# The loads of the down weights of the list of expert units go out from ACT's queue instead of SyncE's

## The reference

```python
def swiglu(h, w_gate, w_up, w_down):
    return (jax.nn.silu(h @ w_gate) * (h @ w_up)) @ w_down
...
    _, eidx = lax.top_k(masked, TOP_K)            # 8 of 64 experts for each token
    ...
    routed = routed_experts(xf, eidx, wts, w_e_gate, w_e_up, w_e_down)
    return routed + swiglu(xf, w_s_gate, w_s_up, w_s_down)
```

## Time and profile before

| | |
|---|---|
| median of 3 runs | 3423.13 us (3420.48 to 3427.93) |
| the profiled execution's own time | 3420.63 us |
| span of its records | 3418.5 us |
| mean granted TensorE clock | 0.869 of full speed |
| PE busy | 2907.1 us (85%) |
| DVE, ACT, POOL busy | 926.5, 652.5, 170.2 us |
| read from HBM, written | 604.84 MB, 47.71 MB |

### The profile page before, as it was taken

The page is one execution under the profiler, slowest core; times in us unless marked ns, Lnnn a source line. Parts: engine busy times, 40 slices in busy tenths (PEclk is TensorE's granted clock), DMA queues, the critical chain, the costliest instruction groups (busy, mean ns, idle before and its releaser), DMA issues.

```text
span 3418.5 us, 39374 instructions
## 1 busy us (share of the span) xinstructions
PE 2907.1 (85%) x16028; PEld 1537.9 (45%) x16028; DVE 926.5 (27%) x2134; ACT 652.5 (19%) x1282; POOL 170.2 (5%) x178
## 2 busy tenths in 40 slices
PE   6867997888999899989897688897888989887885
PEld 3333344666444544434343334344657874332333
DVE  0232443333111432111112421343343142111113
ACT  2232222221100201111110232222222011111111
POOL 0000000000000011111110000000000001111100
PEclk8998578767999889999999799578778989999997
DMA  5100003212120249999996510002110338999994
GB/s 248 67 1 31 0 25 124 75 75 75 49 77 22 82 191 377 422 395 413 372 409 257 205 55 7 25 25 100 51 75 29 145 141 325 419 422 419 413 410 167
DMA packets 74563, 617.38 MB, mean 181 GB/s; under 512 B 17678, under 2 KB 17678, under 8 KB 32016
## 3 DMA queue, kind: packets, MB, share of 16 engines
q1 hardware_dynamic: 50192, 564.49, 40.6%
q0 software_dynamic: 24192, 50.39, 3.9%
HBM read 604.84 MB, written 47.71 MB: 191 GB/s over the span
## 4 chain that ended last, share of the span: by engine, by line
PE 77%; DVE 12%; issue 4%; DMA 3%; ACT 3%; SPq 0%; DVEq 0%; POOLq 0%; ACTq 0%; POOL 0%
PE bank L1595 18%; PE bank L1610 8%; PE bank L1081 7%; PE bank L271 7%; PE bank L342 3%; PE bank L1096 2%; PE bank L1086 2%; PE bank L1585 2%; PE bank L562 2%; PE bank L570 2%; DMA arena<-expert_rows 2%; PE bank L363 1%; PE bank L383 1%; PE bank L401 1%; PE bank L792 1%
## 5 line engine op out<-in xcount | busy, mean ns | idle before, releaser
L1595 PE MATMUL bank<-ring,arena 128*64 128x512 f32 (+1 forms) x1648 | 587.1, 631 | 101.4 <-issue 96.7
L1595 PEld LDWEIGHTS bank<-ring,arena 128*64 128x64 f32 (+1 forms) x1648 | 203.6, 158 | 423.6 <-issue 422.5
L1081 PE MATMUL bank<-normed,ring 128*128 128x512 f32 (+1 forms) x768 | 255.5, 486 | 0.0
L1595 PE MATMUL bank<-branches,arena 128*64 128x512 f32 (+1 forms) x528 | 249.8, 629 | 0.0
L1773 DVE TENSOR_TENSOR arena<-bank,arena 128x256 f32<-128x256 f32 x83 | 35.2, 425 | 705.0 <-ACT arena L1697 705.0
L271 PE MATMUL bank<-normed,ring 128*128 128x512 f32 x512 | 223.4, 598 | 1.3 <-DVE branches L477 1.3
L1519 POOL DMA_INDIRECT arena<-hidden_rows,block_slots x81 | 82.2, 1015 | 2800.4 <-DVE block_slots L1348 2194.4
L1081 PEld LDWEIGHTS bank<-normed,ring 128*128 128x128 f32 x768 | 145.9, 190 | 102.2 <-issue 92.3
L1610 PE MATMUL bank<-ring,arena 128*64 128x512 f32 (+1 forms) x560 | 163.4, 597 | 1.3 <-DVE arena L1779 1.3
L1697 ACT ACTIVATE arena<-bank 128x256 f32<-128x256 f32 x83 | 31.9, 384 | 687.6 <-PE bank L1595 687.6
L271 PEld LDWEIGHTS bank<-normed,ring 128*128 128x128 f32 x512 | 98.1, 192 | 123.9 <-issue 122.1
(11 more groups left out here) (369 smaller groups left out, 4077.3 us busy)
## 6 DMA issues: line engine op xcount, KB each, us to landing
ring<-in_wexp SPq DMA_DIRECT2D x96, 2048.0 KB, 11.1
ring<-in_wst SPq DMA_DIRECT2D x54, 2048.0 KB, 7.7
branches<-in_wexp SPq DMA_DIRECT2D x34, 2048.0 KB, 11.5
ring<-in_wexp SPq DMA_DIRECT2D x66, 1024.0 KB, 11.1
arena<-in_wexp SPq DMA_DIRECT2D x64, 1024.0 KB, 21.5
arena<-expert_rows SPq DMA_DIRECT2D x12, 2048.0 KB, 7.4
ring<-in_wst SPq DMA_DIRECT2D x4, 1536.0 KB, 11.3
hidden_rows<-arena SPq DMA_DIRECT2D x6, 512.0 KB, 3.0
```

Source lines behind the costliest of these rows:

```text
L1081: last = nc.tensor.matmul(ps[2 * (n % 4)][:, c0:], wg[:, k, i * P:(i + 1) * P], H[:, k, c0:], start=(k == 0), stop=(k == KD - 1))
L1595: last = nc.tensor.matmul(ps[2 + s][r0:r1, :], XT_[:, s, k * P + r0:k * P + r1], wt[:, k, :], start=(k == 0), stop=(k == KD - 1))
```

## The change

SP no longer issues the down loads of the list. ACT does: after it has copied the hidden values of unit u, it goes through the down loads whose slot was last used by unit u-1, and for each reads the expert's number, waits for down of unit u-1 and issues the DMA. The first four experts' down loads, those of the loop behind the list and the shared expert's remain on SP. ACT has one more wait ahead of the list, for the ranking (`ro["end"]`), which it must have before it reads `EJI`. Slots, semaphores, sizes and the waits' values are the same.

```diff
             for last_use, kind, p in at.loads:
-                e = sp.value_load(EJI[0:1, p:p + 1], min_val=0, max_val=E)
                 if kind == "gate_up":
+                    e = sp.value_load(EJI[0:1, p:p + 1], min_val=0, max_val=E)
                     sp.wait_ge(un["pe"], after(l, "pe", "gate_up", last_use))
                     gate_up(e, p % 4, gu_in[p % 4])
-                else:
-                    sp.wait_ge(un["pe"], after(l, "pe", "down_right", last_use))
-                    down(e, p % 4, dn_in[p % 4])
...
+            def downs(u):
+
+                for last_use, kind, p in at.loads:
+                    if kind == "down" and last_use == u:
+                        e = act.value_load(EJI[0:1, p:p + 1], min_val=0, max_val=E)
+                        act.wait_ge(un["pe"], after(l, "pe", "down_right", u))
+                        act.dma_start(DN_W[p % 4], wexp[l, bass.ds(e, 1), :, GU_N:].rearrange("a p n -> p (a n)")).then_inc(dn_in[p % 4], 16)
+
+            act.wait_ge(ro["end"], l * RO["end"] + 1)
             rows_in(0)
             for u in range(U):
...
                 copy_hidden(u % 2).then_inc(un["act"], 1)
+                if u:
+                    downs(u - 1)
             rows_out(U - 1)
+            downs(U - 1)
```

## The result

| | before | changed |
|---|---|---|
| median | 3422.06 us (6 runs, 3416.55 to 3427.93) | 3441.35 us (6 runs, 3434.83 to 3447.10) |
| ratio | | 1.0055, 95% interval 1.0039 to 1.0071 |
| profiled execution | 3420.63 us, span 3418.5 | 3434.83 us, span 3432.8 |
| mean granted clock | 0.869 | 0.868 |

What follows compares the result with a forecast made beforehand. It took layer 0 as balanced between PE and DMA and layer 1 as bound by bytes. Terms: 3420.6 + 2.5 + 0.7 = 3423.8 us on the profiled execution, 3426 as a median; range 3401 to 3438.

Steps and rivals of the forecast that it cites:

- rival (b): Layer 0, line 1615: POOL's queue starves; with layer 1's 5.0, 20 us slower, 3441 (3443 as a median); chance 0.26.
- What bounds the kernel: Layer 0's list balanced between PE and DMA, its stalls explained by work, not order alone; layer 1's bound by bytes.
- Part 1: Layer 0: gate and up loads no longer stand behind down loads; taken alone, -26.5 us.
- The 6.1 us for the lower clock: Layer 0: gate_up's extra time at the slower clock behind the stalls, to be removed with the 20.4 us of waits.
- Part 2: Layer 0: gathers lose turns to a third queue, PE's waits move from weights to rows; +2.5 us, bounds -26.5 and +5.0.
- 8 turns of 0.62: A gather's 8 rows an engine each wait for one 16 KB weights row: 5.0 us, close to 5.4 observed.
- the up to 10 us for clock and many short stalls: Layer 0: added up to 10 us if waits return as many short stalls, each bringing a spell of lower clock.
- the arithmetic of the reserve: Layer 0: work that can be put off before PE stops, 9.9 us of rows against 14.9 of weights; shrinks by up to 5.0.
- The 17.4 us of demand in a unit of 11.6: Layer 0: a gather and a scatter occupy POOL's queue 17.4 us per 11.6 us unit while both weight queues are full.
- Part 3: Layer 1: down loads may pass gate and up loads, +5.0 at most; loop's loads issued earlier, -3.4 at most; middle +0.7 us.
- Part 4: Issuing down loads on SP or ACT: SP gains nothing, ACT's 2.2 us are hidden in idle time; 0 us.
- its 5.0 for layer 1: Layer 1: a pair of down loads passes a pair of gate and up loads, at most 2.1 MB, 5.0 us, once.

Runs made afterwards that it cites:

- g3: Layer 0's same units in another order, units of two experts spread, against the kernel before, on one weights' queue: 3402.79 us, ratio 0.9934.
- f3: Layer 0's down loads sorted one unit later (2.3 in place of 1.3), against the kernel before, on one queue: 3440.08 us, ratio 1.0052.
- f2: The kernel before, weights on one queue, with expert weights in HBM as 4 KB pieces with 512 B between them: 3458.38 us, ratio 1.0095.
- g2: The changed kernel, three queues, with expert weights in HBM as 4 KB pieces with 512 B between them: 3458.99 us, ratio 1.0107.
- e2: The changed kernel with the list's down loads on ACT's queue in layer 0 alone, on SP's in layer 1: 3427.88 us, ratio 1.0017.
- e1: The changed kernel with down loads issued by SP again; ACT still reads experts' numbers and waits: 3425.92 us, ratio 1.0012.
- g1: Kernel before with layer 1's down loads on ACT's queue, except the last two, on SP ahead of the loop's loads: 3420.74 us, ratio 0.9993.
- e3: The changed kernel with the list's down loads on ACT's queue in layer 1 alone, on SP's in layer 0: 3429.92 us, ratio 1.0025.
- e4: The changed kernel with weight rows written as 4 KB pieces in the access patterns, which were joined again: 3436.83 us, ratio 1.0038.

## Why the prediction was wrong

It said 3426 us, range 3401 to 3438, with faster 0.24, same 0.43, slower 0.33. The median is 3441.35: past the range, within rival (b), whose price was 3443.

What bounds the kernel: right in the main. DMA's share was 1.00 over layer 1's list and 0.92 over layer 0's, and g3 shows that layer 0's stalls go when the heavy units are spread. f3 doesn't bear on it, as said.

Part 1, the order among the weights: right as a mechanism, the four waits went to zero. The 6.1 us for the lower clock did not come back: PE's busy time in the list rose by 3.0 us.

Part 2, the gathers: what was forecast is what the traces show, rows late and PE's waits moved to them. One of its premises was misread: the 5.3 us of the earlier trace rows are a gather of line 1557, behind the list. The shortest of line 1519 took 7.5 us, so the difference to the median is 3.2 us and not 5.4, and it doesn't match 8 turns of 0.62. That the queues take turns by rows rests on f2 and g2 instead. Off was the size, and with it the choice of the likeliest. I took half of a bound of 5.0 us and left out of the sum the up to 10 us for clock and many short stalls. Layer 0 lost 4.9, 7.6 and 9.1 us in the three profiles with the third queue, 5.8 in e2's median, where the sum had 2.5: at the bound or past it, so the arithmetic of the reserve isn't borne out. Two of its terms are open. The 17.4 us of demand in a unit of 11.6 hold where all rows are filled; with 4096 rows of 6144, as the prediction has them elsewhere, it is 11.6, a queue that just keeps up. And some of the loss may be ACT's waits (2.8 us in e1's profile). I also estimated a gather's latency at 12.7 us, as if each were alone in its queue; it was 41.5, close to the four units (46 us) ahead of which gathers are issued, at which PE stops to wait.

Part 3, the end of layer 1: this is the step that failed, by the largest amount. I wrote that the loop's gate and up loads "now pass that wait, and they share with the down loads ahead of them", and priced it as a gain of up to 3.4 us. The down loads (of unit 30's slots; the prediction says 31) are not ahead of them any more: SP, which no longer stops for down of unit 30, issues the loop's loads about 5 us before ACT issues the down loads that PE needs first. Removing a wait from a queue also removes the order that it gave. Measured: 8.9 us of waiting at down, the list 9.4 us longer and the loop behind it 2.2 shorter, where the term was +0.7 in a range of -3.4 to +5.0; and g1 returns all of it.

Part 4, the issues on ACT: within the measurement. ACT's sigmoid still follows PE after 6.64 us of idle time (1471.33), e1 bounds the cost of the waits at 0 to 9 us with 3.8 as its middle, and g1, with 56 of the 116 loads issued by ACT, has an upper end of +0.7 us; 0 was my term.

The range: its upper end cut through (b), although the prediction's own 17.4 against 11.6 spoke for (b)'s condition. That (b)'s price of 3443 is near the 3441 measured is luck in part: its 10 us for clock weren't seen as such (the granted clock of layer 0's list was 0.98 before and after; PE's busy time rose by 3.0), and its 5.0 for layer 1 were for another event, a pair of down loads that passes gate and up loads in the middle of the list. Of the 15.4 us between the forecast and the median, 2.4 to 3.3 are part 2 (4.9 or 5.8 in place of 2.5), some 7 are part 3 (7.8 in e3's median in place of 0.7); the remaining 5 to 6 are not assigned: e4, the same kernel, stood 4.6 us less above its own before.

## What to carry to other kernels

A transfer that is moved to another queue changes three orders, not one: that among the moved and the left, that of the queue that shares the engines (here small rows of an indirect DMA, which landed after 41.5 us and not 10.7), and that which the moved waits gave to what stood behind them. The third was the surest loss here, and two loads put back removed it: before a wait is taken off a queue, list what stands behind it. Where DMA engines are full, compute each queue's demand in turns against the time per unit; by these runs the one that can't be served is late, however small its bytes, which doesn't say yet what its lateness costs. And where loads are bound by work, reorder the work: spreading the heavy units gave 0.66%, what no order of queues tried here gave.

## What the runs showed of the hardware

- A gather of up to 128 rows of 4 KB landed after 10.7 us beside one queue of 16 KB rows, 7.5 us beside one of 4 KB pieces, 7.6 us beside two queues of 4 KB pieces and 41.5 us beside two of 16 and 8 KB, in the same list of units. Three queues share by pieces, or by packets of so many pieces, and not by bytes; that is how these four figures are read best, with the reserve made above on the gaps in HBM. The Trainium skill ("DMA: Bandwidth & Descriptors", section "Queues, rings and completion order") says that each engine goes round its queues and takes a whole packet, typically 9 to 17 descriptors, from one before it goes to the next. The runs agree with the round; whether a turn is one row or a load's 8 rows an engine, they don't tell. They add that the size of the others' pieces decides what a small queue gets.
- The Trainium skill's rule ("DMA: Bandwidth & Descriptors", section "Issuing engines are not separate DMA queues") that starting DMAs on several engines only saves issue time holds for the total rate (layer 1 of g1, 0.9993) and not for the order: the same bytes on another queue cost 15 to 19 us here, and about 8 us of that by two loads alone.
- A contiguous row written as four pieces in the access pattern reached the engines as one (e4: 16704 packets on q10 as without). With 512 B between pieces in HBM it stayed cut, and the same bytes took some 3% longer (layer 1's list 521.8 for 506.5 us).
